# Two sparse expert layers in one fp32 kernel: query projection before its norm with pipelined heads, a scatter in four banks, and expert rows placed by slot

## The reference

```
xs = h[idx]                                  # 64 tokens an expert
hid = silu(xs @ w_gate) * (xs @ w_up)        # 1024 -> 1024
y = (hid @ w_down) * vals;  x[idx] += ga2 * y
```

```
x = x + softmax(q k^T / sqrt(128)) v @ wo    # q = rmsnorm(x) @ wq
```

## Time and profile before

| | us |
|---|---|
| median of 3 runs (1970.17 to 1977.76) | 1971.36 |
| the profiled execution's own time | 1976.2 |
| its span | 1974.4 |
| PE busy | 1766.4 (89%) |
| DVE busy | 553.2 (28%) |
| ACT busy | 388.9 (20%) |
| POOL busy | 24.6 (1%) |

### The profile page before, as it was taken

One profiled execution on the slowest core, in us unless ns is written; L12 is line 12 of the kernel. 1 busy time (PEld: TensorE's weight loads), 2 busy tenths in 40 slices (PEclk: granted clock), 3 DMA queues, 4 the chain that ended last, 5 costly groups with the idle time before them and its releaser, 6 DMA issues.

```text
span 1974.4 us, 18214 instructions
## 1 busy us (share of the span) xinstructions
PE 1766.4 (89%) x7079; PEld 801.5 (41%) x7079; DVE 553.2 (28%) x1092; ACT 388.9 (20%) x705; POOL 24.6 (1%) x26
## 2 busy tenths in 40 slices
PE   6998999999989999999999799978999988666982
PEld 4544545554445444334443244423444434332320
DVE  4506205541142011111011409753011122520111
ACT  5012114431031101001100300165200004210112
POOL 0000000000000000000000000000000000020002
PEclk9998999999999999999999899978999998887986
DMA  9311444112315999999999312201112111579856
GB/s 368 98 43 43 154 166 170 43 64 85 128 43 219 410 416 421 416 425 424 420 419 415 140 43 85 85 1 43 43 43 85 43 42 43 224 270 339 299 193 179
DMA packets 93577, 374.65 MB, mean 190 GB/s; under 512 B 9716, under 2 KB 10052, under 8 KB 83012
## 3 DMA queue, kind: packets, MB, share of 16 engines
q1 hardware_dynamic: 87108, 350.13, 46.0%
q0 software_dynamic: 2880, 10.49, 2.1%
q10 hardware_dynamic: 3520, 13.10, 1.7%
HBM read 467.02 MB, written 10.49 MB: 242 GB/s over the span
## 4 chain that ended last, share of the span: by engine, by line
PE 81%; DMA 7%; DVE 5%; ACT 4%; SPq 2%; issue 2%; POOL 0%; ACTq 0%; DVEq 0%; POOLq 0%
PE bank L1594 46%; PE bank L1919 11%; PE bank L1944 5%; PE bank L1892 3%; PE bank L1970 3%; DMA weight_slots<-in_expert_w_up 2%; PE bank L2158 2%; PE bank L2172 2%; DMA R<-in_expert_w_down 2%; DMA weight_slots<-in_w_ada 1%; DMA H<-y_rows,token_slot 1%; PE bank L2052 1%; DMA H<-in_w_down_e 1%; PE bank L614 1%; DVE SM L622 1%
## 5 line engine op out<-in xcount | busy, mean ns | idle before, releaser
L1594 PE MATMUL bank<-H,weight_slots 128*128 128x512 f32 (+1 forms) x1088 | 453.6, 577 | 4.0 <-ACT H L650 2.9
L1594 PEld LDWEIGHTS bank<-H,weight_slots 128*128 128x128 f32 x1088 | 210.2, 194 | 245.1 <-issue 236.8
L1594 PE MATMUL bank<-R,weight_slots 128*128 128x512 f32 x576 | 250.8, 596 | 4.4 <-DVE R L1201 2.1
L1594 PEld LDWEIGHTS bank<-R,weight_slots 128*128 128x128 f32 x576 | 109.6, 191 | 142.6 <-issue 135.6
L1919 PE MATMUL bank<-weight_slots,SM 128*64 128x512 f32 x640 | 141.8, 593 | 6.8 <-DVE xT L1264 5.9
L2158 PE MATMUL bank<-weight_slots,SM 128*32 128x512 f32 x768 | 94.3, 636 | 28.1 <-DMA weight_slots<-in_expert_w_up 28.1
L1944 PE MATMUL bank<-weight_slots,SM 128*64 128x512 f32 x384 | 111.8, 594 | 1.6 <-DMA H<-in_w_down_e 1.6
L1594 PE MATMUL bank<-R 128*128 128x128 f32 (+2 forms) x720 | 96.2, 288 | 3.2 <-ACT R L908 2.1
L1594 PEld LDWEIGHTS bank<-R 128*128 128x128 f32 x720 | 87.0, 196 | 7.1 <-issue 4.6
L1919 PEld LDWEIGHTS bank<-weight_slots,SM 128*64 128x64 f32 x640 | 45.3, 137 | 100.3 <-issue 86.8
L1594 PE MATMUL bank<-weight_slots,H 128*128 128x512 f32 x192 | 82.9, 592 | 0.0
(11 more groups left out here) (397 smaller groups left out, 1518.1 us busy)
## 6 DMA issues: line engine op xcount, KB each, us to landing
weight_slots<-in_expert_w_gate SPq DMA_DIRECT2D x102, 512.0 KB
weight_slots<-in_expert_w_up SPq DMA_DIRECT2D x102, 512.0 KB
R<-in_expert_w_down SPq DMA_DIRECT2D x51, 1024.0 KB
weight_slots<-in_w_up_e SPq DMA_DIRECT2D x24, 2048.0 KB, 13.5
...
```

What stands on the lines that cost most here:

```text
L1594: ins = nc.tensor.matmul(dst, lhsT, rhs, start=(i == 0), stop=(i == len(pairs) - 1))
```

## The change

- *First experts.* The scatter uses banks 4 to 7 in turn. The gather is in two halves, the second after expert 1's transposes; the transposes of the weighted selection wait only for the bank that they overwrite. PE waits for all of the scatter before the first `turn`, no longer before expert 1.
- *Cross-attention.* ACT writes `x * gain` (without the norm's factor) into `H` as soon as a tile of `xT` is ready, and the squares beside it; PE sums the squares one by one between the tiles of `w2o`. Queries are computed from the un-normed `H`, and DVE multiplies each head's result with the reciprocal root. Heads are pipelined: scores of head h stand between the query products of later heads, the shares are scaled on DVE, and values follow per head.
- *Router.* No norm `n5`: the router's weights carry the gain (multiplied once, before the first pair), its product reads `xT`, and the factor is applied to the 20 logits. The tokens are turned to rows from `xT`, the first half inside `xa_wo`; DVE evacuates, ACT sums the squares by row. The search for blocks and row places is shorter and gives each token its two places (`token_slot`); the number of the token of each row is no longer computed. The routing weights come after the tables.
- *Rows.* POOL zeroes `x_rows` in DRAM early in the program (from `C0`, which ACT overwrites later and therefore waits for). It then scatters each token's row to its two places (8 scatters of 128 rows), and ACT's queue loads quads in order, four ahead, as four DMAs of 32 rows, and stores results as four DMAs. The gain is applied when the rows are turned. Results are stored unweighted; the last gathers don't accumulate, and DVE adds them with the weights.
- *Weights.* The first expert weights of the second layer are asked for in the order in which their slots come free, down weights partly earlier.

```diff
--- before.py
+++ after.py
...
+                if h == 0:
+                    act.wait_ge(sem("rows_blank"), 16 * NQUAD)
                 act.activation(C0[:, :, h, :], PS[2 + h % 2][:, 0:258].rearrange("p (e d) -> p e d", e=2), ACT.Copy).then_inc(sem("C0_ev"), 1)
...
-            wide_squares(act, "n4", lambda k: act.wait_ge(sem("x3"), k + 1), 4)
...
+            for k in range(KD):
+                act.wait_ge(sem("x3"), k + 1)
+                if k >= 2:
+                    act.wait_ge(sem("rms_sum"), KD * NORMS["n4"] + k - 1)
+                act.activation(xa_sq[:, k % 2, :], xT[:, k, :], ACT.Square).then_inc(sem("rms_sq"), 1)
+                act.activation(H[:, k, 0:T], xT[:, k, :], ACT.Copy, scale=v("xa", k)).then_inc(sem("xa_in"), 1)
+            act.activation(small[:, 44:45], small[:, 40:41], ACT.Sqrt)
+            act.wait_ge(sem("rms_sum"), KD * NORMS["n4"] + KD)
...
+            act.wait_ge(sem("rms_fold"), WIDE["n4"])
+            act.activation(std[:, 0:T], PS[4][:, :], ACT.Sqrt, bias=small[:, 40:41], scale=1.0 / D).then_inc(sem("rms_std"), 1)
...
-            wide_squares(act, "n5", lambda k: act.wait_ge(sem("x4"), k + 1), 4)
...
+            def load_rows(q):
+                by_step = x_rows.rearrange("(c q r) d -> q c r d", c=NSLOT, q=NQUAD)
+                for c in range(NSLOT):
+                    act.dma_start(rows_in[q][BLK * c:BLK * (c + 1), :], by_step[q, c]).then_inc(sem(f"rows_in{q % 4}"), 16)
+
+            act.wait_ge(sem("rows_out"), 16 * 2 * TT)
+            for q in range(4):
+                load_rows(q)
...
+                if q + 4 < NQUAD:
+                    load_rows(q + 4)
...
+            dve.wait_ge(sem("wsmall_in"), 80)
+            nc.vector.tensor_tensor(wsmall[:, :, 40:60], wsmall[:, :, 40:60], v("moe", 0, KD).unsqueeze(2).broadcast_to([P, KD, 20]), ALU.mult).then_inc(sem("router_w"), 1)
...
-                nc.vector.scalar_tensor_tensor(out=xT[:, j, :], in0=PS[2 + j % 2][:, :], scalar=mods[:, 40 + j, 0:1], in1=xT[:, j, :],
+                nc.vector.scalar_tensor_tensor(out=xT[:, j, :], in0=PS[4 + j % 4][:, :], scalar=mods[:, 40 + j, 0:1], in1=xT[:, j, :],
...
-            rms_scale(dve, "n4", lambda k: xT[:, k, :], lambda k: H[:, k, 0:T], T, std[:, 0:T], rstd2[:, 0:T], lambda k: v("xa", k))
...
+            nc.vector.reciprocal(rstd2[:, 0:T], std[:, 0:T]).then_inc(sem("rms_out"), 1)
...
+                nc.vector.tensor_tensor(q2[:, h, :], PS[h][:, :], rstd2[:, 0:T], ALU.mult).then_inc(sem("xq_ev"), 1)
...
+                    nc.vector.tensor_scalar(Px[:, h, i, :], Px[:, h, i, :], xrec[:, h, i:i + 1], None, ALU.mult).then_inc(sem("xP_ready"), 1)
...
+            queries(0)
+            queries(1)
+            maxima(0)
+            shares(0)
+            queries(2)
+            maxima(1)
+            shares(1)
+            queries(3)
+            maxima(2)
...
+            tt(rt["log"], PS[1][:, 0:80].rearrange("p (t n) -> p t n", t=TT), x_rstd4.unsqueeze(2).broadcast_to([P, TT, 20]), ALU.mult)
+            tt(rt["log"], rt["log"], PS[1][:, 80:100].unsqueeze(1).broadcast_to([P, TT, 20]), ALU.add)
...
+            nc.vector.tensor_scalar(token_slot[:, 0:TT], pos2[:, 0, :], -1.0, 0.0, ALU.add, ALU.max).then_inc(sem("token_slots"), 1)
...
-            nc.vector.tensor_tensor(in_row, iota2.unsqueeze(1).broadcast_to([P, 2 * TT, P]), row_of.unsqueeze(2).broadcast_to([P, 2 * TT, P]),
-                                    ALU.is_equal).then_inc(sem("one_hot"), 1)
-            dve.wait_ge(*reached("idx_mm", 1))
-            nc.vector.tensor_copy(slot_token[:, :], PS[4][:, 0:NQUAD]).then_inc(sem("slot_tokens"), 1)
...
+            def add_experts(t):
+                for a in range(2):
+                    if a == 0:
+                        dve.wait_ge(sem(f"y_in{t}"), 16 * 2)
+                    else:
+                        dve.wait_ge(*reached("out_sum", 2 * t + 1))
+                    nc.vector.scalar_tensor_tensor(out=x_tok2[:, t, :], in0=y_in[a][:, t, :], scalar=wt2[:, a, t:t + 1], in1=x_tok2[:, t, :],
+                                                   op0=ALU.mult, op1=ALU.add).then_inc(sem("out_sum"), 1)
...
-            def gather_rows(q):
-                if q >= 2:
-                    pool.wait_ge(sem(f"rows_in{q % 2}"), 16 * (q // 2))
-                nc.gpsimd.indirect_dma_start(rows_in[q], None, h2_rows, bass.IndirectOffsetOnAxis(ap=slot_token[:, q:q + 1], axis=0)).then_inc(sem(f"rows_in{q % 2}"), 16)
...
+            nc.gpsimd.memset(row_zeros, 0.0).then_inc(sem("zeros_by_pool"), 1)
+            pool.wait_ge(sem("zeros_by_pool"), 2)
+            pool.wait_ge(sem("h_ready"), 2 * KD)
...
+                nc.gpsimd.dma_start(x_rows[P * q:P * (q + 1), :], row_zeros).then_inc(sem("rows_blank"), 16)
...
+                pool.wait_ge(*reached("token_slots", a + 1))
+                for t in range(TT):
+                    pool.wait_ge(*reached("h_rows", t + 1))
+                    nc.gpsimd.indirect_dma_start(x_rows, bass.IndirectOffsetOnAxis(ap=token_slot[:, TT * a + t:TT * a + t + 1], axis=0),
+                                                 h2_stage[:, t, :], None).then_inc(sem("rows_out"), 16)
...
+                    nc.gpsimd.indirect_dma_start(y_in[a][:, t, :], None, y_rows, bass.IndirectOffsetOnAxis(ap=token_slot[:, TT * a + t:TT * a + t + 1], axis=0)).then_inc(sem(f"y_in{t}"), 16)
...
-                    if j >= 2:
+                    if j >= 4:
                         pe.wait_ge(sem("sc_v"), done(j))
-                    nc.tensor.matmul(PS[2 + j % 2][:, :], ypair[:, 128 * j:128 * (j + 1)], GT, start=True, stop=True).then_inc(sem("sc_mm"), 1)
+                    nc.tensor.matmul(PS[4 + j % 4][:, :], ypair[:, 128 * j:128 * (j + 1)], GT, start=True, stop=True).then_inc(sem("sc_mm"), 1)
 
...
+                pe.wait_ge(sem("sc_v"), pair * 8 + 16)
                 turn(0)
                 if pair is not last:
-                    gather(pair + 2)
+                    gather(pair + 2, 0)
                 turn(1)
-
-                pe.wait_ge(sem("hidT_ev"), pair * 2 + 2)
+                if pair is not last:
+                    gather(pair + 2, 1)
+                pe.wait_ge(sem("hidT_ev"), pair * 2 + 1)
                 pe.wait_ge(sem("gc_v"), pair + 1)
                 for t in range(TT):
                     ins = nc.tensor.transpose(PS[4][:, 128 * t:128 * (t + 1)], gc[:, t, :, :], ident)
                 ins.then_inc(sem("gt_mm"), 1)
+                pe.wait_ge(sem("hidT_ev"), pair * 2 + 2)
                 for rows in range(2):
...
+                product(b[:, :], [(w[:, k, c:c + 128], merged[:, k, :]) for k in range(KD)]).then_inc(sem("w2o_mm"), 1)
+                if j:
+                    squares_sum("n4", j - 1, part, xa_sq[:, (j - 1) % 2, :])
...
+            query(0, range(7))
+            squares_sum("n4", KD - 1, part, xa_sq[:, (KD - 1) % 2, :])
+            query(0, range(7, KD))
+            query(1, range(2))
+            pe.wait_ge(sem("rms_part"), WIDE["n4"])
+            nc.tensor.matmul(take(4, "rms_std", NORMS["n4"] + 1)[:, :], pick[:, 0:1].broadcast_to([P, P]), sum_parts, start=True, stop=True).then_inc(sem("rms_fold"), 1)
+            query(1, range(2, KD))
+            scores(0)
+            query(2, range(KD))
...
+            def turn_whole(half):
+                for t in range(TT):
+                    b = take(4 + t, "xtok_v", TT * half + t + 1)
+                    for i in range(4):
+                        ins = nc.tensor.transpose(b[:, 128 * i:128 * (i + 1)], xT[:, 4 * half + i, 128 * t:128 * (t + 1)], ident)
+                    ins.then_inc(sem("xtok_mm"), 1)
...
+            for j in range(KD):
+                b = take(j % 4, "x4", j + 1)
+                product(b[:, :], [(w[:, i, 128 * j:128 * (j + 1)], k2[:, i, :]) for i in range(KH)]).then_inc(sem("xo_mm"), 1)
+                if j == 5:
+                    pe.wait_ge(sem("x4"), 4)
+                    turn_whole(0)
+            pe.wait_ge(*reached("router_w", 1))
+            thin_product([(take(0, "thin_ev", 5), slice(0, T))], 40, (sem("x4"), lambda k: k + 1), of=xT)
+            turn_whole(1)
...
+            turn_whole(1)
...
```

563 lines of the change are left out of this document (289 added, 274 removed).

## The result

| median of the runs, us | before | changed | ratio, 95% interval |
|---|---|---|---|
| first comparison (4 and 4 runs) | 1970.86 | 1958.33 | 0.9924 [0.9899, 0.995] |
| the changed kernel again (11 and 5 runs) | 1973.54 | 1958.13 | 0.9922 [0.9897, 0.9947] |

The change makes the kernel faster by 12.5 to 15.4 us. The forecast was 33.6 us, and the range ended at 1956. The sign was right, the size was not.

A forecast was written before the change was run, and what follows sets the result against it. PE bounds most of the chain, with DMA level in the first experts; -0.8 + 0.3 + 6.7 - 17.4 + 2.1 - 16.2 - 2 - 6.3 = -33.6 us gives 1937.8 us against the median, range 1921 to 1956.

The forecast's parts named there:

- Part 1: First experts: scatter in four banks, gather split; -0.8 us, as weights need 59.6 us a pair though PE needs 57.4.
- A: First experts: pairs follow PE as freed buffers let weights come faster, 17 us more saved, 1921 us; chance 0.06.
- D: First experts: waits lower PE's clock, a pair takes 67.5 us, the kernel is slower at 2000 us; chance 0.03.
- Part 2: Second output projection: seven sums of squares between its tiles at 0.95 us each, +6.7 us, range 2.2 to 11.8.
- Part 3: From second output projection to cross-attention's output weights: 52.3 us instead of 69.7, -17.4 us, bounds 46 and 60.
- Rival C: Cross-attention: pipelined heads don't overlap and the squares cost their upper bound, 1955 us; chance 0.12.
- Part 4: Output weights: transposes inside cost +2.1 us; router to first expert product: 37.6 us instead of 53.8, -16.2 us.
- Part 5: Second experts' loop: rows by ACT's queue, issues covered by PE's products, -2 us, bounds -8 and +5.
- Part 6: End: from first of the last gathers 22.6 us instead of 30.9; -6.3 us after 2.0 for the divided last store.
- Part 7: Zeroing the rows in DRAM: twelve early stores are covered, 0 us; 15 us if that cover were gone.
- Rival B: Row scatter: each scatter goes only when the one before has landed, +30 us, 1968 us; chance 0.06.
- signs of being wrong: Pair period near 57.4; POOL issues over 2 us apart; clock under 0.95 in pairs; loop over 5 us beyond 197.

The follow-up runs named there:

- experiment 6: Changed kernel with half of each up weight piece of the first experts not loaded: 1952.08 us, not comparable; pair period 57.17 us.
- experiment 9: Changed kernel with the first experts' scatter back in two banks: 1954.77 us in one run.
- experiment 2: Changed kernel with the squares of the cross-attention's norm added up on DVE instead of PE: 1949.11 us, ratio to before 0.9882.
- Experiment 5: Changed kernel with the second layer's first conditional expert weights held back until the first quad's rows have landed: 1961.27 us.
- experiment 8: Changed kernel with rows numbered by step, so each quad's load and store is one DMA of contiguous rows: 1952.4 us, ratio to before 0.9884.
- experiment 10: Changed kernel with squares added on DVE and rows numbered by step: 1944.06 us; then also products of constants keeping PE busy: 1937.02 us.
- experiment 11: Changed kernel with the last norm's gain product for token tiles 0 and 1 moved to ACT and GpSimd: 1955.48 us; left out: 1958.98 us.

## Why the prediction was right or wrong

*Part 1, first experts:* right. Period 59.64 against 59.6 to 59.9, PE's own 57.2 against 57.4 (experiment 6); the four banks are worth 0.8 (experiment 9). Rivals A and D are out. The ceiling of 435 GB/s of the Trainium skill (DMA: Bandwidth & Descriptors, Where 436 GB/s comes from) gave nothing here: the rate stayed at 422.

*Part 2, squares:* the term was right in kind, 0.95 us each forecast and 1.14 measured, +8.0 instead of +6.7. What I missed is that the term need not exist: on DVE the sums are free (experiment 2).

*Part 3, heads:* 53.4 us, counted behind the seventh sum, against 52.3. Rival C is out: the measured 1958.33 lies near its 1955, but the heads do overlap.

*Part 4, router: the step that failed most, 7.7 us short.* The DVE chain was right (first row places 17.1 us after the output weights against 17.6). Then four terms were undersized: the start of the last issue by 1.2 us, the last scatter's landing by 3.0, the first quad's load with its issues by 3.2, transposes and evacuation by 0.7. My sum hid 0.4 of it: 17.6 + 7 x 1.24 + 4.3 is 30.6, not 31. I priced the landing at the quickest gather, "because the queue is otherwise idle at that time". My queue was, the engines were not: eight scatters of 512 KB, one per 1.25 us, ask for 419 GB/s, near the 422 of this trace, and SyncE adds weights from 1713 on. Experiment 5 puts the price of the weights at 6.0 us. Without them the way from the first scatter to the transposes is 18.5 us, near my 17.8 (35.4 less 17.6), and the last scatter's landing is 0.5 over my 4.3; so the train alone costs little. The range did hold 4.7 of it, but for one DMA; the load had no bound at all. It was right to give little weight to what the Trainium skill says of DVE's two-port mode (SBUF — State Buffer, A bandwidth-pool intuition that's wrong): only the first issue was long. It began 0.2 us into a DVE step of 0.95 us and took 1.65 us instead of 0.95; in experiment 8 it began 0.7 us into that step and took 1.14.

*Part 5, loop: -2 forecast, nearer +5.* The step that failed is that ACT's issues are hidden by PE's products and that the moved rows only leave DMA time. Against the kernel before, the waits for weights fell by 1.1 us only (35.2 against 36.3 in the mean). The last wait for ACT grew from 1.3 to 2.8 us and the way from the last products to the first gather from 7.8 to 8.6 and 9.9, where I had put 2.0. The cold clock in front of the loop costs 2.1 us in the first 64 products (9.15 us in the change at a mean granted clock of 0.77, 7.07 at 1.00 before and in experiment 10); it was not in my sum. These are 3.9 of the 4.8 us, and the loop's own spread is 3. The rows in small pieces cost 6.7 us up to the last products (experiments 8 and 10), which my sum did not price; without them the loop with its last store is 191.9 and 192.5 us, 3.5 under the mean of before, near my -2.

*Part 6, end:* -4.8 instead of -8.3. I followed only the last tile's additions; DVE serves all four tiles, and twelve steps of 1.3 us in a row are longer than the gathers (experiment 11).

*Part 7, zeroing:* right. The twelve stores begin at 48.8 us, and ACT's first copy into `C0` at 234.2 waits for PE, not for them.

*Rival B* is out as put (POOL issues stay 0.3 us apart), but its place was right.

Of my signs of being right, the pair period and the heads came true, the 37 us (45.3) and the 22 to 25 us (25.9) did not. Of my signs of being wrong, one was met in one of two traces: a loop of 202.6 us.

Where it stays open: the medians give 12.5 and 15.4 us, the traces 17.2. The spread of executions covers that; what grants the clock of 1.00 or 0.93 between 1313 and 1427 was not found.
